# Three projection units made token by token, and a new order of VectorE's work in the solve beside attention

## The chip, the cores and the metric

One core of a Trainium2 chip runs the whole program. The metric is the device time of one execution in microseconds, and the median of several executions is compared. The core has TensorE (PE; its weight loads are shown as PEld), VectorE (DVE), ScalarE (ACT), GpSimd (POOL) and SyncE (SP, which issues most transfers here). Each works through its own instructions in order, and they wait for each other by semaphores.

## What is computed

One inference step of a layer for 512 prompt tokens and 8 samples of 16 new tokens, all f32: a SwiGLU feed-forward, a mixer, a second feed-forward, a final norm. The change lies in the mixer. One projection `w_in` feeds two branches:

```
aq, ak, av, iq, ik, iw, gq, gk, gv, gz, gb, ga = split(h @ w_in)
# sparse attention
score = sum_heads(iw * relu(iq . ik));  idx = top_k(score, n_top)
p = softmax(where(valid, q . k_sel + bias, -inf));  attn = p @ v_sel
# gated delta net, in chunks of 64
a = I + strict_lower((k * beta) k^T * decay)
u, w = triangular_solve(a, [v * beta, k * beta * exp(gc)])
per chunk:  v_new = u - w S;  o = q exp(gc) S + qk v_new;  S = S exp(g_last) + k^T v_new
out = concat(attn, rms_norm(o) * silu(gz)) @ w_out
```

The values `av` (256 columns), the key of the index `ik` (64), its weights `iw` (8) and the gates `gb`, `ga` (8) are also needed with tokens on the partitions.

## The kernel before

**Tiles.** The 640 tokens are NT = 5 tiles of 128 (four of the prompt, one of the samples). `h` is held with features on the partitions, KD = 8 tiles deep, as two f32r parts `h_hi` and `h_lo`; weights are split the same way, on ScalarE (`split_hi`, L342) and on VectorE or POOL (`split_lo`, L347). A product of two split operands takes three passes, hi with hi, hi with lo and lo with hi.

**Projection.** `IN_UNITS` (L140) lists 26 units of at most 128 columns of `w_in`: 4 `iq`, 1 `ik`, 3 `tm`, 12 `g` (the convolution), 4 `aq`, `ak`, 4 `gz`, `ak`. SP loads a unit's weights into one of RAW = 2 places (`mix_loads`, L1529) as soon as the place has been split; ScalarE splits AHEAD = 3 units ahead into one of HL = 4 slots. `project` (L3372) holds 128 x 128 of weights and streams `h` past them, 8 x 3 x 2 matmuls of 320 columns each, into one of two PSUM pairs; unit `u` takes `pair[u % 2]` and waits until ScalarE has given it back (`pair_free`). The three `tm` units are `av` in two halves and `ik`, `iw`, `gb`, `ga` in the third. ScalarE copies each from PSUM to a buffer (L1712), TensorE turns it by 5 transposes behind the next unit (L2552), ScalarE copies the turned block to `v_tok` or `small` (L1719, L1720, L1722). Behind the third, in the first `g` unit, ScalarE computes exponentials of the gates (L1727 to L1731) ahead of the evacuation of that unit (L1736). POOL writes `v_tok` and `small` to memory (L1590 to L1593) and splits the low parts of the later `g` units.

**The solve beside attention.** After the projection, attention works on 24 jobs: 16 pairs of prompt heads (jobs 0 to 15, four to a tile) and 8 samples. Each job is: logits on TensorE (L2975, L2978), bias and minimum on VectorE (`biased`, L2495), exponential on ScalarE (L1982), division by the sum on VectorE (`normed`, L2502, L2503), transposes of the probabilities (`turn`, L3035; for samples L3028, L3029), a copy on ScalarE (`turned`, L2005; for samples L1997, L1998), the product with the values of the job before (L3049, L3065). The chunked solve is woven in by hand, in the same order on each engine: `level(x, lv)` takes one doubling step of the inverse for one batch of tiles `x` (0: the samples' tile, 1: tiles 0 and 1, 2: tiles 2 and 3; `LEVELS = (4, 6, 6)`) beside one job. A level is a product on TensorE (L2687; L2685 for level 0), a mask on VectorE (`level_masked`, L2256), up to two more products (L2699, L2704) and additions to `inv_t` and `inv` on VectorE (`level_added`, L2264 for level 0, else L2269 and L2275). The next level's product waits for the addition to `inv_t`.

During batch 0 (four iterations, jobs 0 to 3) VectorE also makes the matrices of each tile (`matrices`, L2230 to L2235), the scaled keys (`keys_in`, L2240) and, at `level_begun(1)` (L2246, L2247), the masked matrix and the first inverse with which batch 1 begins. The top-k of the samples is 8 rounds of MAX8 and MATCH_REPLACE8 on VectorE (`sample_rounds`, L2045, L2049), put between. `w_out(q)` (L2281) copies the w of a tile from PSUM. VectorE's order for a level is

```
level_masked(x, lv); biased(j); before(); normed(j); between(); level_added(x, lv); after()
```

with the parts that the calls of `level` name. Before the change the third and fourth iteration of batch 0 are: masked, biased, a round, normed, added, keys, matrices; then masked, biased, normed, matrices, `level_begun(1)`, added, keys, a round. Two rounds follow, and one as the `before` of level (1, 0), whose `between` is `w_out(0)`.

**The last sample.** On ScalarE `beside_sample` does the exponentials of job j, a `part`, the copy of the turned probabilities of job j - 1, then `after`. In the last one the `part` is `b_out(3)` (L1832, copies of the state's additions) and `o_square(3)` (L1848). VectorE sums the square (`o_squares`, L2330), norms the last job, and adds to the state (`state_step`, L2303), on which TensorE's product at L2792 waits.

Of the kernel before, what the change touches and what calls it, by code (L numbers as in the profile page):

```python
# [20 lines left out]
ACT = mybir.ActivationFunctionType  # L21
# [3 lines left out]
P = 128  # L25
D = 1024
KD = D // P
# [176 lines left out]
def encoder_step(nc, a):  # L204

    ctx = ExitStack()
    with ctx:
# [1137 lines left out]
        iw_x = v_beta[:, 0, 0]  # L1345
        TM_W = (P, P, AD + IDX_HEADS + 2 * GH)

        def tm_f(i):

            return relu_s[:].rearrange("p a b -> p (a b)")[:, 0:TOK] if i == 1 else conv_acc[:, 0:TOK]  # L1350

# [34 lines left out]
        S = {}  # L1386
        for n_ in ("mix_in ik_in evac tm_turned tm iqz rows_turned hist conv conv_kept g_silu "
                   "v_turned v_placed tbl_mm tbl tbl_out gate_in gate_exp g_ready cums cums_out "
# [120 lines left out]
        def mix_loads(sp):  # L1509
# [4 lines left out]
            for v, (kind, i) in enumerate(IN_UNITS):  # L1514
                u = U_IN + v
                dst = w_raw[:, u % RAW]
                sp.wait_ge(lo_done, u + 1)
                if kind == "aq":
                    pr, r = divmod(i, 2)
                    parts = [(g_ * AD, AD, W_AQ + (4 * pr + 2 * g_ + r) * AD) for g_ in range(2)]  # L1520
                elif kind == "ik":
                    parts = [(0, AD, W_IK), (AD, AD, W_IK)]
                elif (kind, i) == ("tm", 2):
                    parts = [(0, 72, W_IK), (72, 8, W_GB)]
                else:
                    parts = [(0, P, {"iq": W_IQ, "tm": W_AV, "g": W_GQ, "gz": W_GZ, "ak": W_AK}[kind] + i * P)]
# [29 lines left out]
        def wait_extra(act, u):  # L1556

            if u in TWO_PARTS:
                act.wait_ge(S["raw_extra"], 16 * (TWO_PARTS.index(u) + 1))
            elif U_OUT <= u < U_FFN2:  # L1560
                act.wait_ge(S["raw_extra"], 16 * (len(TWO_PARTS) + 4 * (u - U_OUT + 1)))

        TWO_PARTS = [U_IN + v for v, (k, i) in enumerate(IN_UNITS) if k in ("aq", "ik") or (k, i) == ("tm", 2)]

        def mix_pool(pool):
# [20 lines left out]
            put_history(1)  # L1586
            pool.wait_ge(S["tm"], 3)
            v_p, v_s = a["_v_p"][0, 0].rearrange("(n p) g d -> p n (g d)", p=P), a["_v_s"][0].rearrange("b t g d -> (b t) (g d)")
# [91 lines left out]
        def mix_act(act):  # L1680
# [4 lines left out]
            for v, (kind, i) in enumerate(IN_UNITS):  # L1685
# [5 lines left out]
                if (kind, i) == ("ak", 1):  # L1691
# [4 lines left out]
                    act.activation(e_out[:], g_sum[:, 1], ACT.Exp).then_inc(S["exps"], 1)  # L1696
                    act.activation(e_end[:], e_end[:], ACT.Exp).then_inc(S["exps"], 1)
                act.wait_ge(unit_done, u + 2)
                if kind in ("iq", "ik", "gz", "aq", "ak"):
# [10 lines left out]
                elif kind == "tm":  # L1710

                    link(act.activation(tm_f(i).rearrange("p (a b) -> p a b", a=2)[0:TM_W[i]], pair[p][0:TM_W[i], :, 0:HALF], ACT.Copy))  # L1712
                    act.sem_inc(S["evac"], 1)
                    act.sem_inc(pair_free[p], 1)
                if v > 0 and IN_UNITS[v - 1][0] == "tm":
                    j_ = IN_UNITS[v - 1][1]
                    act.wait_ge(S["tm_turned"], j_ + 1)
                    if j_ < 2:
                        act.activation(v_tok[:, 0:4, j_ * P:(j_ + 1) * P], hd(0), ACT.Copy)  # L1719
                        act.activation(v_tok[:, 4, j_ * P:(j_ + 1) * P], bank[1][:, 0:P], ACT.Copy).then_inc(S["tm"], 1)  # L1720
                    else:
                        act.activation(small[:].rearrange("p t c -> p (t c)"), bank[3][:, 0:NT * 80], ACT.Copy).then_inc(S["tm"], 1)  # L1722
                if kind == "g" and i == 0:
                    act.wait_ge(S["tm"], 3)

# [62 lines left out]
        def delta_act(act, exps, turned, values_out, keys_ready, sample_rows_out, mixed_samples):  # L1788
# [164 lines left out]
            split_hi(act, U_OUT)  # L1953
            beside_sample(both((b_out, 3), (o_square, 3)))
            turned(N_JOBS - 1, 0)
# [77 lines left out]
        def mix_dve(dve):  # L2033
# [83 lines left out]
            for v, (kind, i) in enumerate(IN_UNITS):  # L2117
# [10 lines left out]
                if (kind, i) == ("tm", 2):  # L2128
# [3 lines left out]
                    for par in range(2):  # L2132
# [4 lines left out]
                        ins.then_inc(S["iqz"], 1)  # L2137
                    dve.wait_ge(S["tm"], 3)
                    link(dve.tensor_scalar(iw_s[:], small[:, :, 64:72], IDX_HEADS ** -0.5, None, ALU.mult))
# [85 lines left out]
        def delta_dve(dve, link, sample_rounds, sample_mask, biased, normed, place_own):  # L2225
# [217 lines left out]

            level(2, 0, None, None, lambda: w_out(1))
            level(2, 1, None, lambda: maps(0))
# [66 lines left out]
        def mix_pe(pe, project, project_two, project_mixed):  # L2512
# [3 lines left out]
            def conv_rows_and_table(part):  # L2516
# [10 lines left out]
                if b:  # L2527
                    pe.wait_ge(S["tbl"], 1)
                pe.matmul(bank[3][0:AH, 0:HALF], rel_w[:], one_hot[:, b * HALF:(b + 1) * HALF], start=True,
                          stop=True).then_inc(S["tbl_mm"], 1)  # L2530

            for v, (kind, i) in enumerate(IN_UNITS):
                u = U_IN + v
                if v >= 2:
                    project(u, 0, (h_hi, h_lo), width=TM_W[i] if kind == "tm" else P)
# [5 lines left out]
                if v > 0 and IN_UNITS[v - 1][0] == "tm":  # L2541

                    j_ = IN_UNITS[v - 1][1]
                    wd = TM_W[j_]
                    pe.wait_ge(S["evac"], v)
                    pe.wait_ge(S["hist"], 3)
                    pe.wait_ge(S["tbl"], 2)
                    if j_:
                        pe.wait_ge(S["tm"], j_)
# [17 lines left out]
                if 0 <= v - SCORE_V < N_DOTS // PER_STEP:  # L2567
                    if v == SCORE_V:
                        pe.wait_ge(S["evac"], V["iq", 3] + 1)
                        pe.wait_ge(S["evac"], V["ik", 0] + 1)  # L2570
# [889 lines left out]
```

## Time and profile before

| | us |
|---|---|
| median of 3 runs (lowest, highest) | 1476.86 (1474.53, 1477.38) |
| the profiled execution, its own time | 1477.88 |
| its span, first to last instruction | 1476.1 |
| first of the 26 projection units to the last | 514 to 775 |
| solve beside attention | 775 to 958 |

The profile is one execution. Times of rows are microseconds from the start of the span; a timeline row has start, length, engine, line, operation, names and shapes, and in brackets the idle time of the engine before it and what ended that. Matmuls overlap, so the distance between starts is what one costs, not its length.

### The profile page before, as it was taken

What the parts mean: (1) busy time and instruction counts of PE and PEld (TensorE: products, weight loads), DVE (VectorE), ACT (ScalarE), POOL (GpSimd) and SP (SyncE); (2) the same over time, 40 slices, a digit from 0 to 9 for tenths busy, and PEclk for the clock granted to TensorE, in tenths of its full rate; (3) what the DMA queues carried; (4) which work ended last, traced back from release to release, by engine and by line L of the source; (5) the groups of instructions that cost most, each with busy time, mean ns of one, the idle gap of its engine ahead of it and who ended that gap; (6) DMA issues with size and microseconds to landing.
All of it is one profiled execution on the core that took longest, in us unless ns stands there. A gap on an engine that the chain in (4) does not pass through costs nothing. (4 is left out here: it accounts for less than half of the span.)

```text
span 1476.1 us, 29079 instructions
## 1 busy us (share of the span) xinstructions
PE 1425.7 (97%) x11722; PEld 1341.4 (91%) x11722; DVE 895.5 (61%) x1648; ACT 568.0 (38%) x1123; POOL 388.7 (26%) x352
## 2 busy tenths in 40 slices
PE   5999999999999999999999899899999999999997
PEld 5999999999999899998896677698999999999997
DVE  5546775675576552676568675654557358754864
ACT  5423331341233443544325434533444124423444
POOL 1603322340341341431002221113632134303400
PEclk9999999999999999999999999999999999999999
DMA  9534543545453233232106031242213213331231
GB/s 340 175 120 129 164 151 115 168 150 157 139 160 103 72 72 90 72 72 61 40 17 150 2 92 42 68 118 56 72 51 109 70 58 87 100 100 38 78 101 71
DMA packets 206618, 148.79 MB, mean 101 GB/s; under 512 B 18075, under 2 KB 190396, under 8 KB 206488
## 3 DMA queue, kind: packets, MB, share of 16 engines
q1 hardware_dynamic: 203320, 137.54, 31.2%
q0 software_dynamic: 3168, 9.42, 2.3%
q8 instruction: 93, 1.52, 0.4%
q14 instruction: 37, 0.30, 0.1%
HBM read 139.99 MB, written 6.95 MB: 100 GB/s over the span
## 5 line engine op out<-in xcount | busy, mean ns | idle before, releaser
L1163 PE MATMUL pair<-b_hi,w_hi 128*128 128x320 f32 x720 | 224.3, 311 | 0.0
L1163 PE MATMUL pair<-b_hi,w_lo 128*128 128x320 f32 x720 | 222.5, 309 | 0.0
L1163 PE MATMUL pair<-b_lo,w_hi 128*128 128x320 f32 x720 | 222.4, 309 | 0.0
L1276 PE MATMUL pair<-act_hi,w_hi 128*128 128x320 f32 x656 | 150.8, 311 | 0.0
L1276 PE MATMUL pair<-act_hi,w_lo 128*128 128x320 f32 x656 | 149.4, 309 | 0.0
L1276 PE MATMUL pair<-act_lo,w_hi 128*128 128x320 f32 x656 | 149.4, 309 | 0.0
L548 DVE SCALAR_TENSOR_TENSOR x_t<-pair,gate,x_t 128x320 f32<-128x320 f32 x120 | 52.5, 479 | 153.7 <-PE pair L1276 128.2
L1163 PEld LDWEIGHTS pair<-b_hi,w_hi 128*128 128x128 f32 x720 | 135.1, 188 | 7.0 <-issue 4.5
L660 ACT ACTIVATE w_hi<-sums_a 128x512 fp32r<-128x512 f32 x72 | 45.1, 626 | 246.3 <-POOL sums_a L694 129.4
L1044 DVE TENSOR_TENSOR uvw<-pair,uvw 128x320 f32<-128x320 f32 (+1 forms) x126 | 67.6, 536 | 115.5 <-PE pair L1163 115.4
L1163 PEld LDWEIGHTS pair<-b_lo,w_hi 128*128 128x128 f32 x720 | 135.2, 188 | 0.0
L1163 PEld LDWEIGHTS pair<-b_hi,w_lo 128*128 128x128 f32 x720 | 135.2, 188 | 0.0
L3372 PE MATMUL pair<-h_hi,w_hi 128*128 128x320 f32 (+1 forms) x544 | 126.4, 314 | 1.3 <-DVEq L560 1.2
L3372 PE MATMUL pair<-h_lo,w_hi 128*128 128x320 f32 (+1 forms) x544 | 123.9, 309 | 0.0
L3372 PE MATMUL pair<-h_hi,w_lo 128*128 128x320 f32 (+1 forms) x544 | 123.9, 309 | 0.0
L1276 PEld LDWEIGHTS pair<-act_hi,w_hi 128*128 128x128 f32 x656 | 109.2, 188 | 3.3 <-issue 2.1
L1276 PEld LDWEIGHTS pair<-act_lo,w_hi 128*128 128x128 f32 x656 | 109.7, 188 | 0.0
L1276 PEld LDWEIGHTS pair<-act_hi,w_lo 128*128 128x128 f32 x656 | 109.6, 188 | 0.0
L3372 PEld LDWEIGHTS pair<-h_hi,w_hi 128*128 128x128 f32 (+1 forms) x544 | 89.7, 187 | 7.9 <-issue 6.4
L666 DVE TENSOR_TENSOR w_lo<-w_raw,w_hi 128x512 fp32r<-128x512 f32 (+2 forms) x90 | 89.6, 996 | 11.3 <-ACT w_hi L660 6.6
L660 ACT ACTIVATE w_hi<-w_raw 128x512 fp32r<-128x512 f32 (+2 forms) x90 | 66.1, 736 | 76.6 <-PE pair L1276 51.2
L660 ACT ACTIVATE w_hi<-raw_more 128x512 fp32r<-128x512 f32 (+2 forms) x90 | 65.7, 736 | 71.9 <-PE pair L1276 56.1
(476 smaller groups left out, 3200.7 us busy)
## 6 DMA issues: line engine op xcount, KB each, us to landing
w_mod_raw<-w_mod SPq DMA_DIRECT2D x28, 1024.0 KB, 6.6
w_raw<-ffn_w_gate SPq DMA_DIRECT2D x40, 512.0 KB, 3.9
raw_more<-ffn_w_up SPq DMA_DIRECT2D x40, 512.0 KB, 3.7
w_raw<-w_in SPq DMA_DIRECT2D x24, 512.0 KB, 3.7
w_raw<-ffn_w_down SPq DMA_DIRECT2D x16, 384.0 KB, 3.5
raw_more<-ffn_w_down SPq DMA_DIRECT2D x16, 384.0 KB, 3.5
w_mod_a<-w_mod SPq DMA_DIRECT2D x4, 1024.0 KB, 10.2
w_mod_b<-w_mod SPq DMA_DIRECT2D x4, 1024.0 KB, 11.3
```

The costliest lines, as they stand in the source:

```text
L548: ins = dve.scalar_tensor_tensor(out=xs, in0=src, scalar=g, in1=xs, op0=ALU.mult, op1=ALU.add)
L660: act.activation(place_of(w_hi_half, w_hi, item), stationary(item), ACT.Copy).then_inc(hi_done, item[4])
L666: dve.tensor_tensor(place_of(w_lo_half, w_lo, item), stationary(item), hi, ALU.subtract).then_inc(lo_done, item[4])
L1044: dve.tensor_tensor(out, bank_ap, other, ALU.add).then_inc(combined, 1)
L1163: mm = pe.matmul(job_bank(j, BANK_OF[part]), w[:, at, kk], mv[:, kk, s], start=(kk == 0 and v == 0 and part in FIRST_OF_BANK), stop=(kk == ...
L1276: mm = pe.matmul(pair[part % 2][:, b, 0:HALF], w[:, slot, k], mv[:, k, b * HALF:(b + 1) * HALF], start=(k == 0 and v == 0), stop=(k == n - ...
L3372: mm = pe.matmul(pair[u % 2][0:width, b, 0:HALF], w[:, 0:width], x_parts[part][:, k, b * HALF:(b + 1) * HALF], start=(k == 0 and v == 0), ...
```

## The change

Four things change. The three `tm` units become one block, `by_tokens`: a tile of `h` is held and the weights of the three units, 112 columns in each of three neighbouring slots, are streamed past it as one moving operand of 336 columns, 24 matmuls for each of the 5 tiles, into banks 0 and 1 by turns. Copies to buffers and transposes go; ScalarE copies each tile to `v_tok` and `small`. All three units end at once, with the last tile. The third unit now has three transfers. On VectorE `level_begun(1)` moves to the third iteration of batch 0, `matrices` and the round of the fourth change places with what was around them, one of two later rounds moves to level (1, 1), and `w_out(0)` and `w_out(1)` go behind `level_added`. On ScalarE `b_out(3)` and `o_square(3)` go behind the copy of the turned probabilities.

```diff
-        TM_W = (P, P, AD + IDX_HEADS + 2 * GH)
+        TM_N = 3
+        TM_W = (AKV * AD + AD + IDX_HEADS + 2 * GH) // TM_N
...
-                elif (kind, i) == ("tm", 2):
-                    parts = [(0, 72, W_IK), (72, 8, W_GB)]
+                elif kind == "tm" and i < 2:
+                    parts = [(0, TM_W, W_AV + i * TM_W)]
+                elif kind == "tm":
+                    parts = [(0, TM_W - 80, W_AV + 2 * TM_W), (TM_W - 80, 72, W_IK), (TM_W - 8, 8, W_GB)]
...
-            pool.wait_ge(S["tm"], 3)
+            pool.wait_ge(S["tm"], NT)
...
+                if (kind, i) == ("tm", 0):
+                    for t in range(NT):
+                        if t < NT - 1:
+                            act.wait_ge(S["tm_mm"], t + 1)
+                        else:
+                            act.wait_ge(unit_done, u + TM_N + 1)
+                        act.activation(v_tok[:, t], bank[t % 2][:, 0:AKV * AD], ACT.Copy)
+                        act.activation(small[:, t], bank[t % 2][:, AKV * AD:TM_N * TM_W], ACT.Copy).then_inc(S["tm"], 1)
                 act.wait_ge(unit_done, u + 2)
...
                 elif kind == "tm":
-
-                    link(act.activation(tm_f(i).rearrange("p (a b) -> p a b", a=2)[0:TM_W[i]], pair[p][0:TM_W[i], :, 0:HALF], ACT.Copy))
                     act.sem_inc(S["evac"], 1)
                     act.sem_inc(pair_free[p], 1)
-                if v > 0 and IN_UNITS[v - 1][0] == "tm":
...
-            beside_sample(both((b_out, 3), (o_square, 3)))
+            beside_sample(None, both((b_out, 3), (o_square, 3)))
...
-                last = lv == LEVELS[0] - 1
-                if not last:
-                    sample_rounds(1)
+                sample_rounds(1)
                 normed(j)
-                if last:
-                    matrices(lv + 1)
-                    level_begun(1)
                 level_added(0, lv)
                 keys_in(lv + 1)
-                if not last:
-                    matrices(lv + 1)
-                if lv in (0, LEVELS[0] - 1):
+                matrices(lv + 1)
+                if lv == 2:
+                    level_begun(1)
+                if lv == 0:
                     sample_rounds(1)
 
-            sample_rounds(2)
-            level(1, 0, lambda: sample_rounds(1), None, lambda: w_out(0))
-            level(1, 1, None, place_own)
+            sample_rounds(1)
+            level(1, 0, lambda: sample_rounds(1), lambda: w_out(0))
+            level(1, 1, lambda: sample_rounds(1), place_own)
...
-            level(2, 0, None, None, lambda: w_out(1))
+            level(2, 0, None, lambda: w_out(1))
...
+            def by_tokens(u):
+
+                slots = slice(u % HL, u % HL + TM_N)
+                pe.wait_ge(lo_done, u + TM_N + 2)
+                pe.wait_ge(S["hist"], 3)
+                for t in range(NT):
+                    if t >= 2:
+                        pe.wait_ge(S["tm"], t - 1)
+                    dst = bank[t % 2][:, 0:TM_N * TM_W].rearrange("p (a n) -> p a n", a=TM_N)
+                    for k in range(KD):
+                        for v, (x, w) in enumerate(((h_hi, w_hi), (h_lo, w_hi), (h_hi, w_lo))):
+                            mm = pe.matmul(dst, x[:, k, cols_of(t)], w[:, slots, k, 0:TM_W], start=(k == 0 and v == 0),
+                                           stop=(k == KD - 1 and v == 2))
+                    if t < NT - 1:
+                        mm.then_inc(S["tm_mm"], 1)
+                mm.then_inc(unit_done, TM_N)
...
-                    for t in range(NT):
-                        dst = (bank[3] if j_ == 2 else bank[0])[:, t * wd:(t + 1) * wd] if j_ == 2 or t < 4 else bank[1][:, 0:P]
-                        mm = pe.transpose(dst, tm_f(j_)[0:wd, cols_of(t)], ident[0:wd, 0:wd])
-                    mm.then_inc(S["tm_turned"], 1)
```

## Rows read from the trace of the kernel before

**Rows 1.** The page, part 1: busy time, share and instructions of each engine.
```profile
PE 1425.7 (97%) x11722; PEld 1341.4 (91%) x11722; DVE 895.5 (61%) x1648; ACT 568.0 (38%) x1123; POOL 388.7 (26%) x352
```

**Rows 2.** Waits of TensorE over the span: total us, times, longest us.
```profile
PE pair L3035 <- DVE logit L2503: 4.0, 2, 2.6
```

**Rows 3.** Stretches: length, busy us per engine (instructions), then granted clock, DMA share, GB/s.
```profile
780.00:800.00 20.00, 18.55 (x236) 12.82 (x236) 17.05 (x45) 11.56 (x32) 6.47 (x8) 1.00 0.95 220
...
820.00:822.00 2.00, 0.61 (x4) 0.40 (x5) 1.72 (x7) 0.87 (x4) 0.00 (x0) 1.00 0.00 0
822.00:824.00 2.00, 1.35 (x19) 1.11 (x21) 1.05 (x2) 1.44 (x3) 0.00 (x0) 0.63 0.00 0
```

**Rows 4.** The chain that ended last: start us, length us, engine and line.
```profile
974.24 42.48 PE pair L3372 x288
...
1445.46 3.16 PE pair L1272 x18
```

**Rows 5.** Timeline of TensorE around the first transposes of the projection.
```profile
568.78 0.71 PE L2552 MATMUL bank<-const,conv_acc 128*128 128x128 f32 x5
569.24 0.53 PE L3372 MATMUL pair<-h_hi,w_hi 128*80 128x320 f32 x2
```

**Rows 6.** Projection: splits, a copy, an evacuation; time to landing of L1529.
```profile
548.08 2.34 DVE L347 TENSOR_TENSOR w_lo<-w_raw,w_hi 128x1024 fp32r<-128x1024 f32 x2
...
DMA to landing us min/median/max: 3.1/3.7/9.4
...
570.36 0.27 ACT L1720 ACTIVATE v_tok<-bank 128x128 f32<-128x128 f32 x1
570.52 1.06 ACT L342 ACTIVATE w_hi<-w_raw 128x1024 fp32r<-128x1024 f32 x1
...
588.24 0.42 ACT L1736 ACTIVATE x_conv<-pair 128x320 f32<-128x320 f32 x1
```

**Rows 7.** Timeline of TensorE: two runs of 64 columns, and one of 128.
```profile
801.14 1.09 PE L2657 MATMUL bank<-qk_f 128*64 128x128 f32 x16
...
915.02 1.09 PE L2792 MATMUL bank<-rel 128*64 128x128 f32 x16
```

**Rows 8.** Timeline of VectorE around the end of batch 0.
```profile
807.03 0.69 DVE L2495 CUSTOM_DVE_ANT_0 logit<-pair,rel 128x512 f32<-128x512 f32 x1 [0.25 <-PE pair L2978]
...
810.03 0.42 DVE L2230 TENSOR_TENSOR m_mat<-decay,m_scale 128x256 f32<-128x256 f32 x1
...
811.62 0.68 DVE L2246 TENSOR_TENSOR decay<-m_mat,const 128x512 f32<-128x512 f32 x1
...
812.95 0.41 DVE L2269 TENSOR_TENSOR inv_t<-inv_t,bank 128x256 f32<-128x256 f32 x1
...
814.13 0.43 DVE L2045 MAX8 mx<-v_f 128x8 f32<-128x272 f32 x1
...
818.46 0.56 DVE L2495 CUSTOM_DVE_ANT_0 logit<-pair,rel 128x384 f32<-128x384 f32 x1 [0.32 <-DVE v_f L2049]
...
821.78 0.68 DVE L2281 COPY k_in<-bank 128x512 f32<-128x512 f32 x1
```

**Rows 9.** Timeline of TensorE: the products of levels (1, 1), (1, 2), (1, 3) and (1, 4).
```profile
823.11 1.97 PE L2687 MATMUL bank<-inv_t,m_mat 64*64 64x64 f32 x32 [0.65 <-DVE inv_t L2264]
...
832.30 1.15 PE L2687 MATMUL bank<-inv_t,m_mat 64*64 64x64 f32 x32
...
841.91 1.15 PE L2687 MATMUL bank<-inv_t,m_mat 64*64 64x64 f32 x32
...
848.76 1.15 PE L2687 MATMUL bank<-inv_t,m_mat 64*64 64x64 f32 x32
```

**Rows 10.** Timeline of TensorE: the product of level (2, 1).
```profile
870.06 1.15 PE L2687 MATMUL bank<-inv_t,m_mat 64*64 64x64 f32 x32 [0.80 <-DVE inv_t L2264]
```

**Rows 11.** Timeline of TensorE and VectorE at the last sample.
```profile
946.77 0.43 PE L3065 MATMUL pair<-v_raw,pt_sb 128*32 128x64 f32 x16 [1.55 <-ACT pt_sb L1998]
...
948.64 0.69 DVE L2303 TENSOR_TENSOR rel<-rel,bank 128x512 f32<-128x512 f32 x1 [1.28 <-PE bank L2780]
```

More of the change, by code:

```diff
@@ L1345, in encoder_step @@
         iw_x = v_beta[:, 0, 0]
-        TM_W = (P, P, AD + IDX_HEADS + 2 * GH)
-        def tm_f(i):
-            return relu_s[:].rearrange("p a b -> p (a b)")[:, 0:TOK] if i == 1 else conv_acc[:, 0:TOK]
+        TM_N = 3
+        TM_W = (AKV * AD + AD + IDX_HEADS + 2 * GH) // TM_N
         tbl = v_f
@@ L1386, in encoder_step @@
         S = {}
-        for n_ in ("mix_in ik_in evac tm_turned tm iqz rows_turned hist conv conv_kept g_silu "
+        for n_ in ("mix_in ik_in evac tm_mm tm iqz rows_turned hist conv conv_kept g_silu "
                    "v_turned v_placed tbl_mm tbl tbl_out gate_in gate_exp g_ready cums cums_out "
@@ L1522, in mix_loads @@
                     parts = [(0, AD, W_IK), (AD, AD, W_IK)]
-                elif (kind, i) == ("tm", 2):
-                    parts = [(0, 72, W_IK), (72, 8, W_GB)]
+                elif kind == "tm" and i < 2:
+                    parts = [(0, TM_W, W_AV + i * TM_W)]
+                elif kind == "tm":
+                    parts = [(0, TM_W - 80, W_AV + 2 * TM_W), (TM_W - 80, 72, W_IK), (TM_W - 8, 8, W_GB)]
                 else:
-                    parts = [(0, P, {"iq": W_IQ, "tm": W_AV, "g": W_GQ, "gz": W_GZ, "ak": W_AK}[kind] + i * P)]
+                    parts = [(0, P, {"iq": W_IQ, "g": W_GQ, "gz": W_GZ, "ak": W_AK}[kind] + i * P)]
                 for n_, (at, wd, col) in enumerate(parts):
@@ L1556, in wait_extra @@
         def wait_extra(act, u):
-            if u in TWO_PARTS:
-                act.wait_ge(S["raw_extra"], 16 * (TWO_PARTS.index(u) + 1))
+            if u in MORE_PARTS:
+                act.wait_ge(S["raw_extra"], 16 * (MORE_PARTS.index(u) + MORE_PARTS.count(u)))
             elif U_OUT <= u < U_FFN2:
-                act.wait_ge(S["raw_extra"], 16 * (len(TWO_PARTS) + 4 * (u - U_OUT + 1)))
-        TWO_PARTS = [U_IN + v for v, (k, i) in enumerate(IN_UNITS) if k in ("aq", "ik") or (k, i) == ("tm", 2)]
+                act.wait_ge(S["raw_extra"], 16 * (len(MORE_PARTS) + 4 * (u - U_OUT + 1)))
+        MORE_PARTS = [U_IN + v for v, (k, i) in enumerate(IN_UNITS) for _ in range(2 if k == "tm" else 1)
+                      if k in ("aq", "ik") or (k, i) == ("tm", 2)]
         def mix_pool(pool):
@@ L1710, in mix_act @@
                 elif kind == "tm":
-                    link(act.activation(tm_f(i).rearrange("p (a b) -> p a b", a=2)[0:TM_W[i]], pair[p][0:TM_W[i], :, 0:HALF], ACT.Copy))
                     act.sem_inc(S["evac"], 1)
                     act.sem_inc(pair_free[p], 1)
-                if v > 0 and IN_UNITS[v - 1][0] == "tm":
[L1716 to L1722, printed above, removed]
                 if kind == "g" and i == 0:
-                    act.wait_ge(S["tm"], 3)
+                    act.wait_ge(S["tm"], NT)
                     act.wait_ge(S["mix_in"], 5 * 16)
@@ L2137, in mix_dve @@
                         ins.then_inc(S["iqz"], 1)
-                    dve.wait_ge(S["tm"], 3)
+                    dve.wait_ge(S["tm"], NT)
                     link(dve.tensor_scalar(iw_s[:], small[:, :, 64:72], IDX_HEADS ** -0.5, None, ALU.mult))
@@ L2530, in conv_rows_and_table @@
                           stop=True).then_inc(S["tbl_mm"], 1)
+            def by_tokens(u):
[13 more added lines that the diff above has]
+                mm.then_inc(unit_done, TM_N)
             for v, (kind, i) in enumerate(IN_UNITS):
                 u = U_IN + v
-                if v >= 2:
-                    project(u, 0, (h_hi, h_lo), width=TM_W[i] if kind == "tm" else P)
+                if (kind, i) == ("tm", 0):
+                    by_tokens(u)
+                elif v >= 2 and kind != "tm":
+                    project(u, 0, (h_hi, h_lo))
                 if v == 2:
@@ L2540, in mix_pe @@
                     conv_rows_and_table(4)
[L2541 to L2549, printed above, removed]
-                    for t in range(NT):
-                        dst = (bank[3] if j_ == 2 else bank[0])[:, t * wd:(t + 1) * wd] if j_ == 2 or t < 4 else bank[1][:, 0:P]
-                        mm = pe.transpose(dst, tm_f(j_)[0:wd, cols_of(t)], ident[0:wd, 0:wd])
-                    mm.then_inc(S["tm_turned"], 1)
                 if v == SCORE_V + 1:
@@ L2568, in mix_pe @@
                     if v == SCORE_V:
+                        pe.wait_ge(S["tm"], NT)
                         pe.wait_ge(S["evac"], V["iq", 3] + 1)
```

## The prediction

> **What bounds the kernel now.** The page comes first: TensorE is busy for 1425.7 of 1476.1 us [rows 1], so time can come from two places only: from columns that TensorE need not stream, and from the 50 us in which it stands still, with the lower clock that a standstill can bring. The waits of TensorE, longest first, show where it stands still; in the mixer the longest is on VectorE's `logit`, 4.0 us in two waits, 2.6 the longer [rows 2]. Stretches of two microseconds show what comes with that wait [rows 3]: TensorE is busy for 0.61 of the 2 us from 820, and in the next stretch the mean granted clock is 0.63: it has gone from 2.4 to 1.2 GHz at about 822.5. The timelines of VectorE and TensorE [rows 8, 9] then give the order in which the work there ends: the reader is to see that VectorE has no gap, and that what TensorE waits for stands behind work that it does not need yet.
>
> **The token-major units.** Today three units of 48 matmuls over 320 columns make values, index keys and small columns. What a matmul costs is not its duration but the distance between neighbours in the chain: 42.48 us for 288 at 320 columns, 147.5 ns each; 3.16 us for 18 at 384 columns (L1272), 175.5 ns [rows 4]. That is 0.44 ns a column, so 336 columns take 147.5 + 16 x 0.44 = 154.5 ns. Removed are 144 x 147.5 = 21.24 us, added 5 tiles x 24 matmuls x 154.5 = 18.54 us: **2.7 us less**. Weights stay 128 columns wide and load beside the matmuls as now, 120 times in place of 144.
>
> Removed too are 15 transposes. The first five begin at 568.78, the next matmul at 569.24 [rows 5]: 0.46 us for five, three times, **1.4 us less**.
>
> Added is a wait. The first convolution unit needs its PSUM pair, and ScalarE gives that back only after it has passed the copies of the last tile and the next weight split, because the three units now end together. If all of these must end first, that is 0.1 us to notice, a copy of 256 columns (at most two of 128, 0.27 each), one of 80 (at most 0.27), a split of 1.06 [rows 6] and 0.1 us back: 2.1 us. If ScalarE only has to issue them, it is little over two crossings between engines, 0.4 us. I take 0.9 us, nearer the lower end: today's split starts 0.16 us after a copy of 0.27 us has started [rows 6], so ScalarE runs ahead of what has not ended. In all **-3.2 us** (-2.0 to -3.7).
>
> What is hidden: all three units' weights must be split before the first tile. The two low splits from 548.08 on end at 550.42 [rows 6]; the first value unit starts two units of 48 matmuls ahead of 568.78, at 554.6. That leaves 4 us for the third transfer of the last unit, issued by SP behind the two others; one of this line lands in 3.7 us (median, 9.4 at most), and SP has nothing else to issue until the next split. ScalarE's copies of a tile fit into the 24 x 154.5 ns = 3.7 us that TensorE needs for one. The weights of convolution units 1 and 2 are split right after the last tile, while unit 0 runs for 7 us. Unit 3's transfer is issued behind the first of these splits, and ScalarE waits for it with the gates' exponentials and the evacuation of unit 0 queued behind: that comes near 585, where it is now at 588.24 [rows 6]. Unit 2 wants the pair near 589, so the cover is 4 us; if that transfer took 9.4 us, 2 us would be lost. POOL's four output transfers wait for the last tile in place of the small columns and go out earlier; nobody waits for them.
>
> **Masks and rounds.** I follow VectorE. In front of the level addition of 812.95 stand the matrices (810.03 to 811.62, 1.59 us) and the masks of batch 1 (811.62 to 812.95, 1.33 us) [rows 8]; 2.92 us go. Into the same path come one round, a third of 814.13 to 818.46, 1.44 us, and the delay that the masks bring from the third iteration: 1.33 less the 0.25 that VectorE stands before the logits of 807.03, 1.1 us. Without cover that makes the addition 0.4 us earlier. But the round now fills the time in which norming waits for ScalarE's exponentials, some 0.6 us of the 1.77 us from the end of the logits (1.23 us after 807.03) to 810.03, since norming by itself takes 1.2 us: **1.0 us earlier**. TensorE needs the fourth iteration's mask, late by 1.1 us too, only behind the products of the next tile. From the addition to the logits of job 4 (818.46) two rounds go (2.89 us) and the matrices come (1.59 us): **1.3 us earlier**. From there norming is as now, and the addition of level (1, 0) then goes ahead of the w copy of 821.78, 0.68 us long and followed by the next after some 0.6: **0.6 us earlier**. The product of 823.11, which waits for that addition [rows 9], starts **2.9 us earlier** (2.3 to 3.0), and TensorE's wait of 2.6 us falls to about 1 us.
>
> So I expect no fall of the clock here. From that product to the next, 823.11 to 832.30, are 9.19 us; two levels on, at full clock, it is 841.91 to 848.76, 6.85 us [rows 9], with about the same work. A round now stands in front of the norming of this job as well, and TensorE waits some 0.1 us for it, or with a copy between up to 0.5 us, which I take off. 9.19 - 6.85 = 2.34, less 0.1: **-2.2 us**.
>
> **The w copy of level (2, 0).** TensorE waits 0.80 us for the addition before 870.06 [rows 10]; the copy in front of it is of the same shape as the one above, 0.6 us, and waits for the product of w besides. Ahead of the copy, the addition ends when the turns do: **-0.7 us**. What needs that w comes a level later.
>
> **The last square.** TensorE waits 1.55 us for ScalarE's copy [rows 11], which stands behind `b_out(3)` and the square. Turned round, TensorE goes on some 0.8 us earlier. But the square then comes later by the copy (0.7 us) and by ScalarE's wait for the turn (0.7 us), 1.4 us in all, and VectorE's sum over it, the norming of the last job and the state addition queue behind it. The addition has a cover of 1.28 us, its wait for TensorE at 948.64 [rows 11]; the rest, and the crossing, is **+0.2 us** (0 to +0.6) for the product that follows it.
>
> **The sum.** -3.2 - 2.9 - 2.2 - 0.7 + 0.2 = **-8.8 us**. The profiled execution took 1477.88 us, its span of 1476.1 included: 1469.1. It lies 1.0 us above the median of 1476.86, from which the same sum gives 1468.1. Between the two I forecast 1468.6 us.
>
> **The rivals.** (a) The clock falls all the same, here or close by. For it: TensorE still has two waits of up to 1 us among small matmuls. Against it: the other wait on `logit`, 4.0 - 2.6 = 1.4 us, lies between 780 and 800, where the clock is 1.00 throughout [rows 3]. It takes the 2.2 us back: 6.6 us gained, 1470.8. (b) The new units give back what they save. The moving operand is now three runs of 112 columns from three weight slots. Beside its columns a matmul costs 147.5 - 320 x 0.44 = 7 ns [rows 4]; three short ones in place of each would add 14 ns x 120 = 1.7 us, and with a release of 2.1 us the units gain 0.3 us, 5.9 in all: 1471.5. With (a) as well 3.7 us are left: 1473.7. (c) Slower: the rate of a moving operand in pieces falls to that of the plain f32 products. Eight of those with 128 columns (two passes each, x16) take 1.09 us [rows 7], 1.06 ns a column; 336 columns would need 357 ns, and 120 x 203 ns are 24 us more: 1493. It decides from 154 + 8800 / 120 = 228 ns a matmul on. Strongly against it: L2657 reads two runs of 64 columns, L2792 one run of 128, and 16 passes of either take 1.09 us [rows 7].
> The Trainium skill says the opposite of that row in "Advanced Engine Details and Errata", PSUM Cachelines: any non-contiguous access pattern slows matmuls significantly. By that rule (c) would be the likely case; the trace does not agree (1.09 us for either form), so (c) keeps little.
> (d) No change that can be told (within 0.2%, 3 us, about what a measurement of this kernel can tell from none): VectorE's new order only moves TensorE's waits from the products to the turns of the jobs, which takes back 2.9 us, and (b) holds: 8.8 - 2.9 - 2.9 = 3.0 us or less, 1474.
>
> **How the numbers follow.** Forecast 0.62; (a) 0.16; (b), alone or with (a), 0.10; (d) 0.07; (c) 0.05. Downwards the bounds allow 0.5 us of the release and 0.2 of the square, and the lowest run shown lies 2.3 us under the median: 1468.6 - 3.0, some 1465.3. Upwards the range takes in (a) and (b), and stops short of both together: 1473.0. Faster by over 0.2% have the forecast, (a) and (b): 0.88; the same 0.07; slower 0.05.
>
> **What would show it.** Right: 120 token-major matmuls some 154 ns apart, a wait of TensorE on ScalarE of about 1 us behind them, no transposes there; the two level products 3 and 5 us earlier against the start of the solve, granted clock 1.00 around them; no wait on `inv_t` at level (2, 0). Wrong: a distance above 200 ns, a half clock in or beside that stretch, a wait of TensorE in the first convolution units, or a longer wait of the last turns on `logit`.

## The result and the profile after

The changed kernel takes **1467.89 us** (median of 4 runs, 1467.54 to 1468.63) against 1477.01 us of the kernel before, measured beside it: a ratio of **0.9949**, 95% interval 0.9937 to 0.9961, so 9.1 us less. Forecast were 1468.6 us and a range of 1465.3 to 1473.0. The profiled execution took 1468.63 us, its span 1466.8.

The page of the changed kernel, part 1, answers to [rows 1]; under it TensorE's waits (total us, times, longest us) that bear on the change, answering to [rows 2] and to the waits in [rows 10, 11].

```profile
PE 1420.5 (97%) x11679; PEld 1336.7 (91%) x11683; DVE 891.8 (61%) x1648; ACT 566.0 (39%) x1125; POOL 389.2 (27%) x352
```

```profile
PE pair L3036 <- DVE logit L2497: 2.5, 3, 1.3
PE pair L3066 <- ACT pt_sb L1996: 1.7, 3, 0.8
PE pair L3029 <- DVE logit L2497: 1.1, 1, 1.1
PE pair L3373 <- ACTq L1720: 0.5, 1, 0.5
```

TensorE is busy for 5.2 us less, the wait of 2.6 us on `logit` is gone, and three things are new: 0.5 us behind the token-major tiles (the PSUM pair, released by ScalarE's queue), a last turn that waits 1.1 us (L3029), and a wait for the copy `pt_sb` that is 0.8 us at most in place of 1.55.

The times at which the same instructions start in the two traces tell where the 9.3 us of span lie. The changed kernel is 1.5 us ahead when the token-major units begin, before any part of the change has run; 4.6 us ahead at the first convolution unit and 4.9 from the second on; 8.1 us at the product of level (1, 1) and 10.6 at that of (1, 2); 11.5 at level (2, 1); 11.7 at the last samples; 10.3 when the projection of the mixed states begins; and 9.3 from the second weights' projection to the end. (The list of units ahead of the prediction adds up to 30, as the trace has it, and not to 26.)

The rows of the level stage, VectorE first, answer to [rows 8]; TensorE's products under them answer to [rows 9].

```profile
801.42 0.68 DVE L2244 TENSOR_TENSOR decay<-m_mat,const 128x512 f32<-128x512 f32 x1
802.14 0.69 DVE L2245 TENSOR_TENSOR inv<-const,decay 128x512 f32<-128x512 f32 x1
...
804.30 0.44 DVE L2043 MAX8 mx<-v_f 128x8 f32<-128x272 f32 x1
...
806.80 0.41 DVE L2267 TENSOR_TENSOR inv_t<-inv_t,bank 128x256 f32<-128x256 f32 x1
...
810.96 0.56 DVE L2489 CUSTOM_DVE_ANT_0 logit<-pair,rel 128x384 f32<-128x384 f32 x1 [0.32 <-DVE v_f L2047]
...
814.27 0.68 DVE L2262 TENSOR_TENSOR inv_t<-const,bank 128x512 f32<-128x512 f32 x1
814.99 0.69 DVE L2279 COPY k_in<-bank 128x512 f32<-128x512 f32 x1
```

```profile
813.88 1.08 PE L3036 MATMUL pair<-const,logit 128*128 128x128 f32 x6 [1.02 <-DVE logit L2497]
815.01 1.15 PE L2688 MATMUL bank<-inv_t,m_mat 64*64 64x64 f32 x32
...
821.66 1.15 PE L2688 MATMUL bank<-inv_t,m_mat 64*64 64x64 f32 x32
...
831.26 1.15 PE L2688 MATMUL bank<-inv_t,m_mat 64*64 64x64 f32 x32
```

The masks (801.42) now precede the round (804.30), and the round, which lasts until 805.40, runs beside ScalarE's exponentials, which end at 805.32. The addition stands 6.15 us before its place in [rows 8], the logits of job 4 7.50, the product of (1, 1) 8.10; each less the 4.93 us by which the whole solve starts earlier. The addition of level (1, 0) goes ahead of the w copy. From product to product are 6.65 us, where [rows 9] have 9.19.

The stretches of the changed kernel (busy us per engine, then the granted clock), to be held against [rows 3]:

```profile
815.00:822.00 7.00, 6.83 (x135) 5.42 (x137) 5.43 (x15) 3.29 (x10) 0.00 (x0) 1.00 0.01 4
...
934.00:937.00 3.00, 1.76 (x32) 1.39 (x32) 1.08 (x4) 1.83 (x4) 0.00 (x0) 0.95 0.00 0
937.00:940.00 3.00, 2.89 (x20) 2.18 (x22) 1.78 (x3) 1.57 (x3) 0.00 (x0) 0.50 0.02 5
```

At the levels the clock stays at 2.4 GHz. A stretch at 1.2 GHz has appeared elsewhere, from 936.7 to 940.1, at the new wait of the last turn. VectorE and TensorE there:

```profile
935.88 0.69 DVE L2328 TENSOR_REDUCE o_ss<-rel 128x4 f32<-128x512 f32 x1 [3.42 <-ACT rel L1846]
...
936.67 0.38 DVE L2497 TENSOR_SCALAR logit<-logit,l_inv 128x304 f32<-128x304 f32 x1
```

```profile
937.11 0.69 PE L3029 MATMUL pair<-const,logit 128*128 128x128 f32 x2 [1.07 <-DVE logit L2497]
```

The turn waits for the norming of the last job, which stands behind VectorE's sum over the last square, which waits 3.42 us for ScalarE. The first question for the experiments is what that costs and whose it is.

### The profile page after: what moved, and what is told of

It reads as the page before. It is cut to its first block and busy times, and to the rows that moved or that the text cites. A ratio compares the mean times of both kernels' runs of the same rounds, so it can differ in the third digit from the quotient of the medians.

```text
span 1466.8 us, 28987 instructions
## 1 busy us (share of the span) xinstructions
PE 1420.5 (97%) x11679; PEld 1336.7 (91%) x11683; DVE 891.8 (61%) x1648; ACT 566.0 (39%) x1125; POOL 389.2 (27%) x352
## 5 line engine op out<-in xcount | busy, mean ns | idle before, releaser
L3373 PE MATMUL pair<-h_hi,w_hi 128*128 128x320 f32 x496 | 115.4, 314 | 1.8 <-DVEq L560 1.2
L3373 PE MATMUL pair<-h_lo,w_hi 128*128 128x320 f32 x496 | 113.0, 309 | 0.0
L3373 PE MATMUL pair<-h_hi,w_lo 128*128 128x320 f32 x496 | 112.9, 309 | 0.0
L3373 PEld LDWEIGHTS pair<-h_hi,w_hi 128*128 128x128 f32 x496 | 82.0, 188 | 8.6 <-issue 7.1
## 6 DMA issues: line engine op xcount, KB each, us to landing
w_mod_a<-w_mod SPq DMA_DIRECT2D x4, 1024.0 KB, 10.2
```

Of the source, the lines that this page charges most:

```text
L3373: mm = pe.matmul(pair[u % 2][0:width, b, 0:HALF], w[:, 0:width], x_parts[part][:, k, b * HALF:(b + 1) * HALF], start=(k == 0 and v == 0), ...
```

## The experiments

Each time is a median with its ratio to the kernel before, measured beside it. There were three such measurements (the kernel before: 1475.96, 1476.53 and 1476.11 us); the ratios, not the times, compare runs of different ones.

**The units alone, and VectorE's order alone.** The first is the kernel before with `by_tokens` and what belongs to it; the second is the kernel before with these lines:

```
-                last = lv == LEVELS[0] - 1
-                if not last:
-                    sample_rounds(1)
+                sample_rounds(1)
...
+                if lv == 2:
+                    level_begun(1)
...
-            sample_rounds(2)
-            level(1, 0, lambda: sample_rounds(1), None, lambda: w_out(0))
-            level(1, 1, None, place_own)
+            sample_rounds(1)
+            level(1, 0, lambda: sample_rounds(1), lambda: w_out(0))
+            level(1, 1, lambda: sample_rounds(1), place_own)
...
-            level(2, 0, None, None, lambda: w_out(1))
+            level(2, 0, None, lambda: w_out(1))
```

Expected of the units:

> The kernel before with the token-major units of the change alone (VectorE's order, the w copies and the last square as before). Theory: the units give 3.4 us, as the distance between the two traces grows from 1.5 us ahead of them to 4.9 us behind the first convolution unit, so 1473.6 us against 1477.0; matmuls of 336 columns some 153 ns apart; the stretch of TensorE from the product of level (1, 1) to that of (1, 2) stays 9.2 us with its fall of the clock. Rival: the 1.5 us by which the changed kernel was ahead at the start of the units belong to the change as well (fewer transfers and instructions), and then the time is 1472.1 us.

Expected of the order:

> The kernel before with VectorE's new order alone (masks of batch 1 in the third iteration, one round in each of three jobs, the w copies of levels (1, 0) and (2, 0) behind the addition); units and last square as before. Theory: 5.7 us up to the product of level (1, 2), 2.3 to 2.6 of which are the clock, and 0.9 at level (2, 0), 6.6 in all: 1470.4 us; product (1, 1) to product (1, 2) in 6.7 us; no wait on inv_t. Rival: the time at the lower clock is only put off to another place, so that some 2.4 us of this are given back later: 1472.8 us, with a stretch at half clock behind 835 us that the kernel before does not have.

Measured: units 1472.31 us, 0.9977 (0.9968 to 0.9986), 3.65 us less; order 1470.35 us, 0.9964 (0.9951 to 0.9978), 5.6 us less. Together 9.3 us against the 9.1 of the whole: within their intervals the parts add up. The units' rival (4.9 us, the head start included) lies outside the interval, 2.1 to 4.7 us: the head start is not theirs. In these two traces it was 0.8 and 1.2 us. The units' trace keeps the fall at the levels (this timeline of TensorE holds the product of (1, 1)); the order's has it no more:

```profile
818.92 1.97 PE L2692 MATMUL bank<-inv_t,m_mat 64*64 64x64 f32 x32 [0.65 <-DVE inv_t L2262]
...
828.03 1.15 PE L2692 MATMUL bank<-inv_t,m_mat 64*64 64x64 f32 x32
```

```profile
818.76 1.15 PE L2683 MATMUL bank<-inv_t,m_mat 64*64 64x64 f32 x32
...
825.40 1.15 PE L2683 MATMUL bank<-inv_t,m_mat 64*64 64x64 f32 x32
```

9.11 us and 6.64 us. The order's median lies between theory (6.6) and rival (4.2), and the interval holds both; its trace decides against the rival as far as it goes: 6.6 us won between the start of the solve and level (2, 1), and no half clock between the levels and 1013 us that the kernel before doesn't have.

**Does a moving operand in pieces cost anything?** One long run, and twelve short ones:

```
-    mm = pe.matmul(dst, x[:, k, cols_of(t)], w[:, slots, k, 0:TM_W], ...
+    mm = pe.matmul(dst, x[:, k, cols_of(t)], w[:, u % HL + k % TM_N].rearrange("p k n -> p (k n)")[:, k % 6 * P:k % 6 * P + TM_N * TM_W], ...
...
+    mm = pe.matmul(dst, x[:, k, cols_of(t)], w[:, slots, k].rearrange("p a (h n) -> p a h n", h=4)[:, :, :, 0:TM_W // 4], ...
```

> The changed kernel with the moving operand of the 120 token-major matmuls as one run of 336 adjacent columns of a single weight slot (values, index keys and small columns are then those of other weights). Theory: three runs of 112 cost nothing, so the matmuls stay 153 ns apart and the time is the changed kernel's 1467.9 us within its spread. Rival, priced in the prediction at 7 ns for each further run: 14 ns x 120 = 1.7 us less, 1466.2 us, the matmuls 139 ns apart.

> The changed kernel with that operand in twelve runs of 28 columns, 4 columns apart (of each slot other columns than the reference's are taken). Theory: columns alone are paid for, 153 ns, 1467.9 us. Rival at 7 ns for each further run: 9 x 7 = 63 ns more, 216 ns apart, 7.6 us more: 1475.5 us.

Measured: 1468.17 us, 0.9941 (0.9924 to 0.9958), and 1468.57 us, 0.9946 (0.9929 to 0.9962): no difference from the changed kernel. The line of the 120 matmuls in the trace of the changed kernel, then of one run, then of twelve (duration min/median/max in ns, first and last start; here the last of their three forms):

```profile
L2537 PE MATMUL bank<-w_lo,h_hi x40: 310/314/315, 553.5 to 571.4; 128*128 128x336 f32 x40
```

```profile
L2537 PE MATMUL bank<-w_lo,h_hi x40: 316/316/317, 554.7 to 572.6; 128*128 128x336 f32 x40
```

```profile
L2537 PE MATMUL bank<-w_lo,h_hi x40: 315/316/316, 553.8 to 571.8; 128*128 128x336 f32 x40
```

First to last of all 120 is 18.25 us in each, 153.3 ns a matmul. Rivals (b), as far as it rests on pieces, and (c) are out. The rule of the Trainium skill that the prediction weighed ("Advanced Engine Details and Errata", PSUM Cachelines) is not borne out for this operand: a run of 28 columns streams as fast as one of 336. The section is about PSUM, though, and this operand lies in SBUF; its destination in PSUM is one stretch of 336 columns in all three kernels, so the rule for PSUM itself was not tried.

**What do masks and rounds carry, each?** In the changed kernel the masks back in the fourth iteration, with the matrices ahead of its addition:

```
                 normed(j)
+                if lv == LEVELS[0] - 1:
+                    matrices(lv + 1)
+                    level_begun(1)
                 level_added(0, lv)
                 keys_in(lv + 1)
-                matrices(lv + 1)
-                if lv == 2:
-                    level_begun(1)
+                if lv < LEVELS[0] - 1:
+                    matrices(lv + 1)
```

> The changed kernel with the masks of batch 1 back in the fourth iteration, together with the matrices ahead of its level addition; the rounds stay spread. Theory: VectorE has almost no gap here, so up to the product of level (1, 1) the order of masks and matrices counts little: that addition comes 1.6 to 1.9 us later, the product of level (1, 1) only 0.2 to 0.4 us later, 1468.2 us, full clock throughout. Rival: TensorE's longer stand at that addition brings the half clock back close by, 2.4 us more: 1470.6 us.

And one round back:

```
-            sample_rounds(1)
+            sample_rounds(2)
             level(1, 0, lambda: sample_rounds(1), lambda: w_out(0))
-            level(1, 1, lambda: sample_rounds(1), place_own)
+            level(1, 1, None, place_own)
```

> The changed kernel with one round moved back from the second job of batch 1 (level (1, 1)) to the place ahead of its first; the masks stay in the third iteration. Theory: this round alone carries half of the gain at the product of level (1, 1): the product 1.4 us later, TensorE's wait ahead of it 2.4 us, and with that the half clock returns beside it, 9 us from that product to the next in place of 6.65: 3.7 us more, 1471.6 us. Rival: the clock holds, the wait being shorter than the 2.6 us of before, and the second job wins 0.1 us: 1469.2 us.

Measured: 1469.99 us, 0.9956 (0.9939 to 0.9973), and 1469.66 us, 0.9955 (0.9938 to 0.9971). The two runs with other operands, measured beside them, stand at 0.9941 and 0.9946, so these lie about 0.001 higher, less than their intervals: the times alone don't tell them from the changed kernel, and the argument rests on the traces. With the masks back, TensorE's timeline and its stretches (granted clock third from the end):

```profile
805.94 1.04 PE L3038 MATMUL pair<-const,logit 128*128 128x128 f32 x8
808.96 1.70 PE L2688 MATMUL bank<-const,decay 64*64 64x64 f32 x32 [1.98 <-DVE inv_t L2267]
...
817.03 1.15 PE L2690 MATMUL bank<-inv_t,m_mat 64*64 64x64 f32 x32
```

```profile
807.00:809.00 2.00, 0.04 (x2) 0.04 (x2) 1.87 (x4) 0.66 (x2) 0.00 (x0) 1.00 0.00 0
809.00:811.00 2.00, 2.00 (x34) 1.60 (x34) 1.55 (x4) 1.14 (x4) 0.00 (x0) 0.58 0.00 0
```

My theory for this run fell, its rival stood: TensorE has no wait there in the changed kernel, now stands 2.0 us at the addition, the clock falls to 1.2 GHz right behind it, and the product of (1, 1) comes 2.4 us later against the instruction before that wait, not 0.3. So moving the masks is worth a wait and a fall of its own, which the prediction's terms hid in "1.0 us earlier".

With the round back:

```profile
817.52 1.07 PE L3036 MATMUL pair<-const,logit 128*128 128x128 f32 x6 [2.51 <-DVE logit L2497]
818.64 1.92 PE L2688 MATMUL bank<-inv_t,m_mat 64*64 64x64 f32 x32
...
826.58 1.15 PE L2688 MATMUL bank<-inv_t,m_mat 64*64 64x64 f32 x32
```

The wait is about as forecast (2.5 us for 2.4), the product 1.5 us later, the half clock is back; but product to product is 7.94 us, not 9: the fall took 1.3 us where the kernel before lost 2.5, as the half clock lasted 3.4 us (818.7 to 822.1) in place of 6.8. The mechanism was right, the price of the clock too high. The time lies nearer the rival's 1469.2 us, but the rival's condition, that the clock holds, did not come.

**The last square: order and norming.** Undone on ScalarE, and, as another cure, VectorE's norming of the last job ahead of its sum:

```
-            beside_sample(None, both((b_out, 3), (o_square, 3)))
+            beside_sample(both((b_out, 3), (o_square, 3)))
```

```
-            beside_sample(both((o_sum, 3), (o_squares, 3)))
-            normed(N_JOBS - 1)
+            beside_sample(lambda: o_sum(3))
+            normed(N_JOBS - 1)
+            o_squares(3)
```

> The changed kernel with the copy of the last square's group and the square put back ahead of ScalarE's last-but-one turned copy. Theory: the new order of the last square costs 1.4 us in the trace (0.8 gained at the values, 1.5 lost to the last turn's wait for the normed logits with its lower rate, 0.2 regained, 0.9 lost to the half clock behind it); put back, that is gone: 1466.5 us, no wait of the last turn on logit, no stretch at half clock near 937 us. Rival, the working on record: the new order costs 0.2 us only, and the clock falls there for another reason: 1467.7 us and the half clock stays.

> The changed kernel with VectorE's norming of the last job moved ahead of its sum over the last square (the sum follows behind it). Theory: the last turn waited 1.1 us because that norming stood behind the sum, which waited 3.4 us for ScalarE's square; ahead of it the wait goes, TensorE does not fall to half clock near 937 us, and the time is 0.8 us under that of the square put back: 1465.8 us. Rival: the sum now stands in front of the state addition, and what the turn wins is lost at the product behind that addition: 1467.5 us.

Measured: 1466.88 us, 0.9944 (0.9930 to 0.9958), and 1465.67 us, 0.9934 (0.9920 to 0.9948). Both traces are without the half clock near 937. Whether that half clock is the kernel's had to be seen beside the changed kernel itself, so these three were measured again, beside each other:

> The changed kernel as it is, a second time, beside the three that follow and on the same chip. Theory and rival both: a ratio of 0.995 to the kernel before, 9 us less or a little over; whether the half clock near 937 us and the longer one ahead of the second weights' projection come again tells whether they belong to the kernel or to one execution.

> The changed kernel with the last square's old order on ScalarE, beside the changed kernel on the same chip. Theory: the new order costs 1.4 us, 0.9 of them by the clock, so this one is 1.0 to 1.4 us under the changed kernel of the same call. Rival, the working on record: 0.2 us under it, no more than the runs spread.

> The changed kernel with the last job's norming ahead of VectorE's sum over the last square, on the same chip. Theory: 2.0 to 2.3 us under the changed kernel (1.1 of the wait, the rest the clock). Rival: what the first measurement showed over 1.4 us was the difference of two calls, and it is 1.2 us or less.

Measured: changed 1467.30 us, 0.9942 (0.9929 to 0.9954); square undone 1466.02 us, 0.9934 (0.9921 to 0.9947); norming first 1466.44 us, 0.9934 (0.9921 to 0.9947). TensorE in the second profile of the changed kernel, then with the square undone, then with the norming first:

```profile
932.61 0.44 PE L3029 MATMUL pair<-const,logit 128*128 128x128 f32 x2
...
934.14 0.43 PE L3066 MATMUL pair<-v_raw,pt_sb 128*32 128x64 f32 x16 [0.76 <-ACT pt_sb L1996]
...
936.97 0.44 PE L3029 MATMUL pair<-const,logit 128*128 128x128 f32 x2 [1.07 <-DVE logit L2497]
...
937.67 1.09 PE L2793 MATMUL bank<-rel 128*64 128x128 f32 x16
...
942.20 1.13 PE L2781 MATMUL bank<-rel,v_par 128*128 128x128 f32 x8 [0.93 <-issue]
```

```profile
933.09 0.44 PE L3029 MATMUL pair<-const,logit 128*128 128x128 f32 x2
...
935.41 0.43 PE L3066 MATMUL pair<-v_raw,pt_sb 128*32 128x64 f32 x16 [1.56 <-ACT pt_sb L1996]
...
942.53 1.13 PE L2781 MATMUL bank<-rel,v_par 128*128 128x128 f32 x8 [0.82 <-issue]
```

```profile
932.76 0.44 PE L3030 MATMUL pair<-const,logit 128*128 128x128 f32 x2
...
934.29 0.43 PE L3067 MATMUL pair<-v_raw,pt_sb 128*32 128x64 f32 x16 [0.76 <-ACT pt_sb L1996]
...
935.89 0.38 PE L3030 MATMUL pair<-const,logit 128*128 128x128 f32 x2
...
937.33 1.09 PE L2794 MATMUL bank<-rel 128*64 128x128 f32 x16 [0.72 <-DVE rel L2301]
...
941.74 1.13 PE L2782 MATMUL bank<-rel,v_par 128*128 128x128 f32 x8 [0.82 <-issue]
```

The same kernel has the same wait of 1.07 us and this time no half clock there; the longer one ahead of the second weights' projection did come again. Six profiles of this study have that wait (both of the changed kernel, both of the operand, masks and round back); four of them show the half clock behind it, none of the eight profiles without the wait does. From the first to the last row of each fence are 9.59 us in the changed kernel, 9.44 with the square undone and 8.98 with the norming first; in the first profile of the changed kernel, with the half clock, it was 10.85 (932.75 to 943.60). So at full clock the new order costs 0.15 us against the square undone, which waits 1.56 us at the values, and norming first wins 0.5. My price of 1.4 us was thus the price of one execution: 0.15 us and, where the clock falls, some 1.3 on top.

The square undone lies 1.3 us under the changed kernel here, as its theory had it; in the two traces, though, only 0.15 us of that lies at the last square, and 1.2 at the half clock ahead of the second weights' projection, which is shorter with the square undone (last section). Norming first lies 0.9 us under it and not 2.0 to 2.3, so there the rival stood. Against the changed kernel neither version is apart by its interval, and the times don't order the two (1466.02 and 1466.44 us here, 1466.88 and 1465.67 before). By its traces norming first is the shortest in this stage.

**One round later still.** On top of norming first:

```
-            level(1, 0, lambda: sample_rounds(1), lambda: w_out(0))
+            level(1, 0, None, lambda: w_out(0))
             level(1, 1, lambda: sample_rounds(1), place_own)
-            level(1, 2, both((sample_mask,), (new_v, 0)))
+            level(1, 2, both((sample_rounds, 1), (sample_mask,), (new_v, 0)))
```

> The kernel with the norming first, and in addition the round in the first job of batch 1 (level (1, 0)) moved to level (1, 2), where TensorE's turns come 2.3 us after VectorE has normed. Theory: TensorE's wait of 1.0 us ahead of the product of level (1, 1) falls to 0.4 and nothing waits in exchange: 0.6 us under the kernel with the norming first. Rival: the round delays the level addition and with it the product of level (1, 3), no gain, the wait only moves there.

Measured: 1468.15 us, 0.9945 (0.9932 to 0.9958), a miss: 0.9 us were won at the turn ahead of the product of (1, 1), 0.3 of them lost again at the next turn, and 2.2 us lost at the product of level (1, 3). The rival named the place; the reason is another. TensorE's turn ahead of that product, VectorE's norming for which it waits, then POOL's work:

```profile
833.09 0.55 PE L3037 MATMUL pair<-const,logit 128*128 128x128 f32 x3 [1.42 <-DVE logit L2498]
```

```profile
828.98 2.09 DVE L2498 TENSOR_SCALAR logit<-logit,l_inv 128x384 f32<-128x384 f32 x1
...
831.17 1.86 DVE L2498 TENSOR_SCALAR logit<-logit,l_inv 128x384 f32<-128x384 f32 x1
```

```profile
828.96 7.69 POOL L1633 TENSOR_TENSOR s_in<-s_in,e_end 128x1024 f32<-128x1024 f32 x4 [45.67 <-PE bank L2816]
```

The same instruction with the norming first, just ahead of POOL's work, which begins at 828.98 there too:

```profile
827.95 0.42 DVE L2498 TENSOR_SCALAR logit<-logit,l_inv 128x384 f32<-128x384 f32 x1
```

The round pushed the norming by 1 us, under POOL's four multiplications of 1.9 us each, and each of its two `TENSOR_SCALAR` then took about as long as one of them. That the one holds up the other is read from these rows; no run was made for it alone.

## Why the prediction was right, and where it was not

**Token-major units: right, 3.4 us for 3.2.** The matmuls are 153.3 ns apart (154.5 forecast), 2.8 us less. TensorE waited 0.5 us for the release; by the starts it cost 0.67 (571.43 to 572.25, less one distance), in place of the 0.9 taken between 0.4 and 2.1: it is near the lower bound, as [rows 6] suggested, and its releaser is ScalarE's queue, not a finished split. What was called hidden was: the late transfer held ScalarE 5.3 us, until 579.49, the convolution's evacuation came at 583.72 (about 585 forecast), and TensorE waited for neither. With the transposes' 1.4 us these sum to 3.5, against 3.4 in the distance between the traces.

**Masks and rounds: right, 3.2 us for 2.9.** Addition 1.2 us earlier (1.0), logits of job 4 another 1.35 (1.3), product another 0.6 (0.6): together just over the upper end of the stated 2.3 to 3.0. TensorE's wait of 2.6 us fell to 1.02, as said. The working was incomplete in one place: it costed the masks as VectorE's time only. Run alone, undoing them brings a wait of 2.0 us at another product and a half clock behind it. What the w copy of level (1, 0) gives by itself was not tried.

**The clock at the levels: right, 2.5 us for 2.2.** Product to product 6.65 us, the wait of this job's turn for the round 0.17. **The w copy of level (2, 0): right**, 0.87 for 0.7.

**The last square: this step failed.** It let the later norming delay only the state addition, covered by 1.28 us [rows 11], and left out that the last turn waits for that same norming. That turn stood 1.1 us: "a longer wait of the last turns on `logit`", one of the prediction's own signs of being wrong. That the balance at full clock is still the +0.2 forecast (0.15) is luck, since the path is another; and the wait brought the half clock in four of six profiles. In the profiled run the stage lost 1.4 us.

**Rival (a)** asked for the half clock "here or close by": not here in any profile of the changed kernel, close by in one of its two. **(b), (c), (d)** are out: no cost of pieces, 0.5 to 0.7 us for the release, and the waits did not move to the turns in the level stage.

**The sum** held partly by luck, because the errors are small and of both signs: 3.4 + 3.2 + 2.5 + 0.9 less 1.4 are 8.6 us against 8.8 forecast. The rest of the 9.3 us of span lies outside the change's steps: 1.5 us at the start, 0.2 at a transfer that TensorE waits for near 924, and 1.0 lost near 1010, where the half clock lasted from 1008.4 to 1018.6 in place of 1020.5 to 1027.3 before.

## What to carry to other kernels

Where one engine is busy all the time but a few microseconds, find the instruction that ends each of its waits and ask what stands ahead of it that nobody needs yet; moved work belongs where the engine that takes it waits anyway, and its new neighbours, another engine's long instructions among them, have to be looked up before it is put there. When an order is turned round, list every consumer of each instruction that comes later, not only the one that the step is about. And a wait of one or two microseconds in a stretch of small matmuls can cost as much again through the clock, in some executions and not in others: one profile doesn't price it.

## What the runs showed that was not expected

**VectorE's norming beside POOL.** `TENSOR_SCALAR` on 384 columns took 0.42 us, and 2.09 and 1.86 us while POOL's multiplications of 1.9 us each ran. The Trainium skill says why this can be, in "SBUF — State Buffer", section "SBUF: two separate sides": VectorE and GpSimd share a port pair that one instruction holds to its end while the other blocks, if VectorE's runs in a two-port mode or reads two inputs from SBUF. The trace agrees, to the length of one POOL instruction for each norming; in which mode the norming ran, no run here shows. VectorE's addition behind them, which reads a PSUM bank, took its usual 0.68 us beside the same work of POOL.

It was there all along. In each of the fourteen profiles the first norming beside POOL's multiplications of `v_beta` takes 1.85 or 1.86 us, the next of the same size 0.49, and TensorE's other wait on `logit`, 1.3 us, ends with the long one. In the kernel before:

```profile
783.32 4.03 POOL L1614 TENSOR_TENSOR v_beta<-v_beta,rn 128x512 f32<-128x512 f32 x4
```

```profile
785.79 1.85 DVE L2503 TENSOR_SCALAR logit<-logit,l_inv 128x512 f32<-128x512 f32 x1
```

```profile
787.70 1.25 PE L3035 MATMUL pair<-const,logit 128*128 128x128 f32 x8 [1.33 <-DVE logit L2503]
```

What moving that work of POOL would give was not tried.

**The clock's price is not fixed.** Behind waits of 2.6 (two profiles), 2.5 and 2.0 us (one each) it fell every time, behind that of 1.07 us in four profiles of six, behind the 1.02 us at the levels in none of nine. The length of a wait alone does not decide it: the clock held behind 1.55 us at the values in the five profiles with the old order of the last square, behind 1.42 us in the last run, and behind the 1.3 us at the first turn in all fourteen. What a fall cost went with how long the half clock lasted: 2.5 us at the levels where it lasted 6.8 us (the kernel before, the units alone), 1.1 to 1.3 us where it lasted 3.4 (the round back, and the four at the last turn).

Ahead of the second weights' projection the half clock lasted 10.2 us in eight of the fourteen profiles and 6.8 in six. From TensorE's first matmul behind its wait of 1.2 us (963.95 in the changed kernel's first profile) to the end of the span that cost the changed kernel's first profile 1.0 us against the kernel before, and its second 1.2 against the square undone and 1.0 against the norming first. All six profiles with the wait of 1.07 us at the last turn are among the eight; whether that order brings the longer half clock was not tried.
